# A four-layer transformer on one core: attention heads that add rotated halves in the contraction, another loading order at the start, and sums of exponentials on GpSimd

## The reference, cut to what matters

```
def apply_rope(x, cos, sin):
    half = x.shape[-1] // 2
    x1, x2 = x[..., :half], x[..., half:]
    return jnp.concatenate([x1 * cos - x2 * sin, x1 * sin + x2 * cos], axis=-1).astype(x.dtype)
...
        s = (jnp.einsum('bqhd,bkhd->bhqk', qn_b, k_nope)
             + jnp.einsum('bqhd,bkd->bhqk', qr_b, k_rope)).astype(jnp.float32) * scale
```

```
    s = jnp.einsum("bshd,bmhd->bhsm", q, k).astype(jnp.float32) * (1.0 / math.sqrt(XA_HD))
    p = jax.nn.softmax(s, axis=-1)
    o = jnp.einsum("bhsm,bmhd->bshd", p.astype(v.dtype), v)
```

## Time and profile before

| | us |
|---|---|
| median of 3 runs (lowest, highest) | 2482.35 (2479.43, 2487.03) |
| the profiled execution | 2481.47 |
| its span, first to last instruction | 2479.7 |
| PE busy | 2331.0 (94%) |
| POOL busy | 1661.9 (67%) |
| DVE busy | 1051.8 (42%) |
| ACT busy | 501.6 (20%) |

### The profile page before, as it was taken

One profiled execution on the slowest core, in us unless ns is written; L12 is line 12 of the kernel. 1 busy time (PEld: TensorE's weight loads), 2 busy tenths in 40 slices (PEclk: granted clock), 3 DMA queues, 4 the chain that ended last, 5 costly groups with the idle time before them and its releaser, 6 DMA issues.

```text
span 2479.7 us, 29722 instructions
## 1 busy us (share of the span) xinstructions
PE 2331.0 (94%) x11040; PEld 1901.3 (77%) x11040; DVE 1051.8 (42%) x1342; ACT 501.6 (20%) x955; POOL 1661.9 (67%) x1370
## 2 busy tenths in 40 slices
PE   5968999999996899999999699999999898999999
PEld 4766788888876678888887468888888776888887
DVE  7664533322366344332237545215334333540430
ACT  3245211110134521111012521001111263100000
POOL 5466677767756667777777577767766564776774
PEclk9988999999998899999999899999999999999999
DMA  4300122222330012222232112222232200222222
GB/s 145 107 27 18 68 102 95 91 87 93 117 107 18 18 69 102 97 89 87 94 124 102 52 68 88 99 102 96 91 119 86 86 35 17 85 102 102 85 102 85
DMA packets 37844, 207.93 MB, mean 84 GB/s; under 512 B 3532, under 2 KB 10316, under 8 KB 16888
## 3 DMA queue, kind: packets, MB, share of 16 engines
q1 hardware_dynamic: 37752, 206.70, 23.9%
HBM read 204.55 MB, written 2.13 MB: 83 GB/s over the span
## 4 chain that ended last, share of the span: by engine, by line
PE 60%; DVE 2%; POOL 2%; ACT 2%; issue 1%; DVEq 0%; POOLq 0%; ACTq 0%
PE ps L821 18%; PE ps L826 18%; PE ps L825 18%; POOL wl L649 1%; PE ps L1185 1%; PE ps L1159 1%; ACT rt L1335 1%; POOL wh L643 0%; PE ps L1160 0%; PE ps L1163 0%; PE ps L1161 0%; DVE sq L1705 0%; DVE t L1713 0%; DVE nt L1705 0%; PE ps L1200 0%
## 5 line engine op out<-in xcount | busy, mean ns | idle before, releaser
L649 POOL TENSOR_TENSOR wl<-raw,wh 128x512 fp32r<-128x512 f32 (+1 forms) x776 | 1032.8, 1361 | 0.0
L643 POOL TENSOR_SCALAR wh<-raw 128x1024 fp32r<-128x1024 f32 (+1 forms) x388 | 427.3, 1121 | 595.3 <-PE ps L821 462.6
L821 PE MATMUL ps<-h,wh 128*128 128x512 f32 x1576 | 618.1, 392 | 18.4 <-POOL wl L649 9.2
L825 PE MATMUL ps<-h,wh 128*128 128x512 f32 x1576 | 615.2, 390 | 0.0
L826 PE MATMUL ps<-h,wl 128*128 128x512 f32 x1576 | 615.1, 390 | 0.0
L821 PE MATMUL ps<-act,wh 128*128 128x512 f32 x1120 | 437.6, 391 | 1.1 <-DVE x L1705 1.1
L825 PE MATMUL ps<-act,wh 128*128 128x512 f32 x1120 | 436.0, 389 | 0.0
L826 PE MATMUL ps<-act,wl 128*128 128x512 f32 x1120 | 436.0, 389 | 0.0
L821 PEld LDWEIGHTS ps<-h,wh 128*128 128x128 f32 x1576 | 297.0, 188 | 85.5 <-issue 24.4
L825 PEld LDWEIGHTS ps<-h,wh 128*128 128x128 f32 x1576 | 296.9, 188 | 62.3 <-issue 1.0
L826 PEld LDWEIGHTS ps<-h,wl 128*128 128x128 f32 x1576 | 297.0, 188 | 62.1
(11 more groups left out here) (337 smaller groups left out, 2681.8 us busy)
## 6 DMA issues: line engine op xcount, KB each, us to landing
raw<-w_gu SPq DMA_DIRECT2D x44, 1024.0 KB, 4.8
raw<-w_up SPq DMA_DIRECT2D x32, 1024.0 KB, 4.8
raw<-w_down_b SPq DMA_DIRECT2D x32, 1024.0 KB, 4.8
raw<-w_down_a SPq DMA_DIRECT2D x32, 704.0 KB, 4.0
raw<-w_in_a SPq DMA_DIRECT2D x14, 1024.0 KB, 4.9
raw<-w_in_f SPq DMA_DIRECT2D x13, 1024.0 KB, 4.8
raw<-w_in_r SPq DMA_DIRECT2D x11, 1024.0 KB, 4.8
raw<-w_out_a SPq DMA_DIRECT2D x8, 1024.0 KB, 7.6
```

The costliest lines, as they stand in the source:

```text
L643: pool.tensor_scalar(hi_s[:, part], raw[s][:, part], 1.0, 1.0, ALU.mult, ALU.mult).then_inc(hi_done, 1)
L649: ins = pool.tensor_tensor(lo_s[:, part], raw[s][:, part], hi_s[:, part].bitcast(F32), ALU.subtract)
L821: first = pe.matmul(out, w_hi, v_hi, start=start, stop=False)
L825: pe.matmul(out, w_hi, v_lo, start=False, stop=False)
```

## The change

Four things are changed.

1. MLA queries keep 128 rows: one multiplication by `cgq` on all rows, no addition. The key's 32 rotated rows stand twice in the 128-row key tiles, so the score matmul adds the two products. One copy (`krp`) is added per layer, and the four zero fills of the key tiles at the start of MLA are gone.
2. High part and rest of a key are one tile `key` of 128x1024, so a zero fill of both is one instruction where SWA and FOX still need it.
3. At the start SP issues `vec`, then the first weight chunk, then `x` in four parts, then the constants, the small tables and the second chunk. ACT makes the row tiles first and copies the constants behind them. POOL splits the first chunk by halves (`half_ready` after the first), and PE's small products for the bias table stand behind `lead_pair`.
4. In XA, POOL adds the two halves of the exponentials (`summed`), and PE multiplies that sum with the ones: one float32 matmul instead of two. POOL's `mixed` of an earlier head stands ahead of the splitting of a chunk in these heads.

```
-                halves = (slice(0, n // 2), slice(n // 2, n))
...
+                if early:
+                    for half in range(2):
+                        pool.wait_ge(hi_done, high(half))
+                        low(2 * half).then_inc(hi_done, 1)
+                        low(2 * half + 1).then_inc(w_ready if half else half_ready, 1)
+                        hi.up()
...
+            def summed(hd):
+                if hd >= 2:
+                    pool.wait_ge(ready[5], bk.filled(5, hd - 2))
+                for b in (2, 3):
+                    pool.wait_ge(free[b], bk.emptied(b, hd))
+                pt = pts["xa"][hd % 2]
+                pool.tensor_tensor(pt_sum[hd % 2], pt[:, 0:T], pt[:, T:2 * T], ALU.add).then_inc(sum_ready, 1)
...
+                    if m.name == "xa":
+                        if hd >= 2:
+                            mixed(m.vrow(hd - 2), m.tile(hd - 2))
+                        if hd < m.heads:
+                            summed(hd)
                     if hd == chunk_at:
 
                         split_all(1, BLOCKS)
...
-                        for j in range(keys):
-                            last = pe.matmul(ps[5][:, :], ones[:, :], pt[:, j * T:(j + 1) * T],
-                                             start=j == 0, stop=j == keys - 1)
-                        last.then_inc(ready[5], 1)
+                        pe.wait_ge(sum_ready, sumr.up())
+                        pe.matmul(ps[5][:, :], ones[:, :], pt_sum[hd % 2], start=True, stop=True).then_inc(ready[5], 1)
...
+                tsc(krp[96:P, :], krp[64:96, :], 1.0)
...
-                    tt(qc[0:96, i, :], ps[b][0:96, :], cgq[0:96, :], ALU.mult)
-                    tt(ts[64:96, :], ps[b][96:P, :], cgq[96:P, :], ALU.mult, bk.empties(b, u))
-                    tt(qc[64:96, i, :], qc[64:96, i, :], ts[64:96, :], ALU.add)
+                    tt(qc[:, i, :], ps[b][:, :], cgq[:, :], ALU.mult, bk.empties(b, u))
...
-                    for s in range(2):
-                        zero(kh[s], slice(96, P))
-                        zero(kl[s], slice(96, P))
-                    r = slice(64, 96)
+                    r = slice(64, P)
                     tt(ts[r, :], krp[r, :], ps[7][r, :], ALU.mult, bk.empties(7, 0))
```

More of the change, by code:

```diff
@@ L435, in build @@
         free = [sem(f"free{b}") for b in range(8)]
-        ld_x, ld_vec, ld_cst, ld_pos = sem("ld_x"), sem("ld_vec"), sem("ld_cst"), sem("ld_pos")
+        ld_x = [sem(f"ld_x{i}") for i in range(KT // 2)]
+        ld_vec, ld_cst, ld_pos = sem("ld_vec"), sem("ld_cst"), sem("ld_pos")
+        half_ready = sem("half_ready")
         ld_hot = sem("ld_hot")
@@ L624, in _, with split @@
             g = 0
-            def split(s, nblk, first=False, slot_done=None):
+            def split(s, nblk, first=False, slot_done=None, early=False):
                 full[s].n += 16
@@ L905, in claim, with bias_rows, in_a @@
                 return tt % 4
-            pe.wait_ge(consts_ready, 1)
-            pe.wait_ge(ld_relb, 16)
-            pe.wait_ge(ld_hot, 16)
-            for half in range(2):
-                pe.matmul(ps[4 + half][0:SWA_HEADS, 0:384], relb[0:32, 0:SWA_HEADS],
-                          cst[0:32, C_HOT + 384 * half:C_HOT + 384 * (half + 1)],
-                          start=True, stop=True).then_inc(ready[4 + half], 1)
-            bk.close({4: 1, 5: 1})
-            def in_a():
+            def bias_rows():
+                pe.wait_ge(consts_ready, 1)
+                pe.wait_ge(ld_relb, 16)
+                pe.wait_ge(ld_hot, 16)
+                for half in range(2):
+                    pe.matmul(ps[4 + half][0:SWA_HEADS, 0:384], relb[0:32, 0:SWA_HEADS],
+                              cst[0:32, C_HOT + 384 * half:C_HOT + 384 * (half + 1)],
+                              start=True, stop=True).then_inc(ready[4 + half], 1)
+                bk.close({4: 1, 5: 1})
+            def in_a(first):
                 lead_pair(claim(0), claim(1), chunk())
+                if first:
+                    bias_rows()
                 norm_sums(True)
@@ L1372, in square_rows @@
                 hr.n += 1
+            sc.wait_ge(ld_vec, 16)
+            for k in range(KT):
+                sc.wait_ge(ld_x[k // 2], 16)
+                if k >= 2:
+                    sc.wait_ge(h_ready, hr.at(-1))
+                fn(h[:, k, 0, :], x[:, k, :], ACT.Copy, scale=col("attn0", k)).then_inc(h_hi_ready, 1)
+                fn(sq[:, k % 2, :], x[:, k, :], ACT.Square).then_inc(square_ready, 1)
+                hr.n += 1
             sc.wait_ge(ld_cst, 16)
-            sc.wait_ge(ld_vec, 16)
             for dst, c0 in ((ident, C_IDENT), (ones, C_ONES), (ident_r, C_IDENT), (anti_r, C_ANTI), (neg_ones_r, C_ONES),
@@ L1382, in _ @@
             last.then_inc(consts_ready, 1)
-            sc.wait_ge(ld_x, 16)
-            for k in range(KT):
-                if k >= 2:
-                    sc.wait_ge(h_ready, hr.at(-1))
-                fn(h[:, k, 0, :], x[:, k, :], ACT.Copy, scale=col("attn0", k)).then_inc(h_hi_ready, 1)
-                fn(sq[:, k % 2, :], x[:, k, :], ACT.Square).then_inc(square_ready, 1)
-                hr.n += 1
             sc.wait_ge(turns_ready, 1)
```

108 lines of the change are left out of this document (60 added, 48 removed).

## The result

The changed kernel takes 2466.74 us (median of 6 runs, 2464.09 to 2474.36); the one before, with three more runs beside it, 2481.76 (2479.43 to 2487.24). The ratio is 0.9940 (0.9929 to 0.9951): 15.0 us less, where 21.7 were forecast. The executions of one kernel are not alike: the six of the changed kernel have mean granted clocks of 0.979 (the shortest, 2464.09) down to 0.970 (the longest, 2474.36). So a stage length read from one trace is that of one execution.

The account below looks back on a forecast made before the run. PE's matmuls carry 60% of the chain, so only places where PE waits can give time. Terms 5.0 + 6.2 + 5.2 + 0.4 + 3.4 + 1.5 = 21.7 off 2481.47 gave 2459.8 us, range 2452 to 2472.

Parts of the forecast that it names:

- rival 1: XA: POOL's sums cost what they save, 0.5 in layer F and 1.5 lost in R; 2465.7 us, chance 0.16.
- rival 2: Layers 0 and 1: POOL's windows take all the MLA query gain, DVE is early and waits; 2466.0 us, chance 0.12.
- rival 4: Start: the new order gains nothing, `cq` is waited for until 55.67 as before; 2464.8 us, chance 0.07.
- A: Start: new loading order and split first chunk bring tile 4 earlier; 5.0 us gained (2.7 to 6.5).
- B: MLA queries, layers 0 and 1: 12 DVE instructions go, POOL's windows hold most; 3.1 us per layer, 6.2 (3 to 8).
- Rival 3: Layers 0 and 1: POOL's windows don't hold, POOL too is freed; 7.3 us per layer, 2451.4, chance 0.06.
- C: Start of MLA: four zero fills leave DVE's queue ahead of `ts`; 2.6 us per layer, 5.2 (4.8 to 6).
- E: XA in layer F: one half of the matmuls with the ones goes, four heads; 3.4 us (0.5 to 3.5).
- F: XA in layer R: same removal, but sums collide with DVE's recurrence; 1.5 us gained (-1.5 to 3.5).
- FOX: FOX: eight zero fills become four of double width; 0.4 us gained (nothing to 1.3).
- (5): Weight blocks behind the broken lead: TensorE stays at 1.2 GHz, kernel slower than before; 2488.6 us, chance 0.02.

Follow-up runs that it names:

- start_only: Kernel before with only the third edit (loading order, first chunk split by halves, bias products behind the lead): 2477.34 us, ratio 0.9982.
- xa_only: Kernel before with only the fourth edit (sums of exponentials on POOL, split results ahead of the chunk): 2477.00 us, ratio 0.9988.
- mla_only: Kernel before with only the first two edits (128-row MLA queries, joined key tiles, no zero fills at MLA's start): 2474.94 us, ratio 0.9976.
- before_filled: Kernel before with all the filling matmuls of best: 2476.03 us, ratio 0.9982.
- prep_between: Changed kernel with POOL's preparation `ql` of the second pair of SWA heads moved between the two window sets: 2469.51 us, ratio 0.9942.
- warm_all: warm_mla with more filling matmuls ahead of SWA's score columns, behind the last MLA head and at FOX's start: 2462.09 us, ratio 0.9914.
- fills_back: Changed kernel with four fills of 32x512 put back ahead of MLA's first `ts`: 2469.18 us, ratio 0.9935.
- warm_mla: Changed kernel with 25 filling matmuls per layer of kind A ahead of the waits at MLA's start: 2462.50 us, ratio 0.9929.
- best: Changed kernel with warm_mla's filling, 8 more behind MLA's and XA's last heads, 6 behind FOX's, layer R's sums on PE: 2452.58 us, ratio 0.9874.
- changed_again: Changed kernel run once more, unaltered, for a second trace: 2466.05 us, ratio 0.9948.
- r_pe_sum: Changed kernel with layer R's sums of exponentials on PE again: 2464.40 us, ratio 0.9926.

## Why the prediction was right, and where its sizes were off

The forecast 2459.8 was 6.9 below the median and the range 2452 to 2472 held it; the direction was right. The time by itself proves little of the mechanism: 2466.74 lies nearer to rival 1 (2465.7), rival 2 (2466.0) and rival 4 (2464.8) than to the forecast, and only the rows below tell them apart. Some of it was luck: the profiled difference of 13.6 holds 1.7 at the start and 2.1 in layer R's inputs that no step of the prediction had and that come and go with TensorE's level; in layer F the level took 1.5 back. By terms:

**A, 5.0: measured 5.5 (5.8 alone) in the traces, 4.4 by start_only's median.** POOL began on the first chunk at 6.55 (6.0 forecast), DVE at 10.69 (10.3), the eighth row ended at 30.15 (30.6), the stall of 2.31 went. The lead ended 1.1 later than I took it, as the seventh row was done at 28.64 and not at 27.3; the lead's last 30 matmuls took 9.0 from there, near the 9.2 forecast, and the first nine of them did run 0.43 apart. So tile 4 came 55.67 - 51.88 = 3.8 earlier. The other 1.7 no step had: before, the wait of 2.31 was followed by 8 matmuls at the low level. They are gone with the wait, but they are also absent in xa_only, mla_only and before_filled, which have the wait: against those traces the new start gains about 4. Before, from tile 4 to `cqn`:

```profile
55.60:74.90 19.30, 19.21 (x77) 14.04 (x78) 14.75 (x15) 6.09 (x10) 10.97 (x9) 0.91 0.16 54
```

and after:

```profile
51.80:69.40 17.60, 17.59 (x79) 12.86 (x78) 14.55 (x15) 4.19 (x7) 11.16 (x9) 1.00 0.23 89
```

**B, 3.1 per layer: 3.2 and 3.1 at the first SWA result.** The first maxima came 7.2 earlier than the shift of the start, 7.3 forecast, and GpSimd's windows took 4 back, as forecast; prep_between and warm_all show that it is that queue. Both parts of the 3.1 are there: the maxima behind `t` start 0.15 after `t` ends instead of 1.6, and POOL's queue from the first `ql` to the second takes 25.3 instead of 27.3, 2.0 less (1.6 forecast). Rival 3 and with it the full effect of the rule in the Trainium skill, "SBUF — State Buffer", section "Who interferes with whom", did not come about, though single rows agree with the rule: DVE's key rest, two inputs in SBUF, is 1.64 beside POOL's split and 0.69 without. Of instructions with two inputs the section says only that they contend; "for the whole instruction" stands there for DVE's two-port modes. POOL won 2.0 per layer, not 6.8. The prediction's reckoning by that rule also mixes its figures: 13.6 is twice 6.8, already below twice 7.3, so rival 3's 30.1 is no cut of 29.1.

**C, 2.6 per layer: 1.6 and 2.0.** This is the term that was mis-sized, and the step is "4 x 0.65 = 2.6 of PE's 5.66, so DVE still is what PE waits for". DVE still was, and the wait fell from 5.66 to 3.07 as forecast; but right behind it, without the fills, DVE's first key rest falls on POOL's split of the fifth SWA result and takes 0.95 longer (fills_back). I had not asked what else ran on POOL at that moment.

**The sum.** B and C together were to stay: 11.4 in two layers. 4.8 and 5.1 arrived at MLA's first heads, less 1.7 that layer 0 lost in the later SWA heads; the residuals kept -0.9 and 3.9. In layer 0, 2.2 went in the MLA heads and 1.7 at the output projection, PE's granted clock being 0.87 and 0.92 there against 0.95 and 1.00. That the level is the cause of these two is shown by warm_mla and best, which do the same work plus filling in 44.55 and 20.23. The prediction treated an earlier start as a gain that stays; it named the level only as a rival behind the lead. The 1.7 of the later SWA heads is the level too. In layer 0 of the changed kernel the score columns of head 2, behind a PE wait of 1.68, fall to 0.21 apart after the first seven matmuls:

```profile
145.63 0.41 PE L1201 MATMUL ps<-ql,key 128*128 128x256 f32 x1
145.85 0.42 PE L1202 MATMUL ps<-qh,key 128*128 128x256 f32 x1
```

and in best, with the same code there and no filling, behind a wait of 0.25, they stay at 0.12:

```profile
145.84 0.28 PE L1210 MATMUL ps<-ql,key 128*128 128x256 f32 x1
145.96 0.28 PE L1211 MATMUL ps<-qh,key 128*128 128x256 f32 x1
```

The slow columns lie across the first SWA result, where the table cuts, so a clock of 0.98 for the stage hides them. In changed_again, warm_mla and r_pe_sum the columns are slow too and the stage takes 25.3; in mla_only, prep_between and best they are not, and it takes 23.6.

**E, 3.4: 3.4,** in the changed kernel and in xa_only (2.5 in the traces of r_pe_sum and fills_back, whose code there is the same); heads 4.98 apart instead of 5.84. **F, 1.5: 0.3,** and -0.9 in xa_only, with the sums themselves costing about 0.9: it lies between the forecast and the bound -1.5, by the mechanism given for that bound. **FOX, 0.4: -0.7** with layer F's inputs; 1.5 of it is a stretch of weight blocks, which no edit touched, at a lower level. The same sort of thing paid 2.1 in the inputs of layer R: the stage is as short in start_only and mla_only and as long as before in xa_only, prep_between and fills_back, and no edit touched it. **Rivals:** of (1) the sums' cost in R was seen, but R as a whole did not lose 1.5 and F paid in full; (2), (3) and (4) did not come about. Of (5) only the level was seen: the lead's matmuls were back at 0.23 after the first ten, and the low level came later, in the heads.

## What to carry to other kernels

A saved wait is a gain at its place only; follow it to the next point where all engines meet, and expect part of it to be taken or doubled there by TensorE's level. Before an instruction is removed as dead weight, look at what the next one will run beside. In a kernel with short broken stretches between long rows of matmuls, filling the waits on TensorE with matmuls into a bank that is about to be overwritten can be worth as much as a tuned change: best, with layer R's sums on PE again, is 14.2 us below the changed kernel, and 1.26% below the one before. But the same filling in the kernel before gave only 4.3, so such filling has to be tried at each place. And read a stage in more than one trace before giving it a price: here the same code differed by 1 to 2 us from trace to trace.

## What the runs showed of the hardware that I had not expected

In the trace of before the granted clock fell some time after a wait, not in it: tile 4's first four matmuls behind the 2.31 of waiting are 0.23 apart, and the next eight 0.43. In three other traces of the same start the clock did not fall there at all. Two traces of the changed kernel agree in the length of every stage of layers 0 and 1 to 0.1 us, levels included, while r_pe_sum, the same program up to layer R, differs by 1.8 in one of them; and six executions of the changed kernel differ by 10 us, the longer the lower their mean granted clock (0.979 to 0.970). Filling does not work everywhere: where the next stage waits for another engine's queue (SWA) it gave nothing, and warm_all, with filling in FOX, has the last products of layer F's heads at the low level, 3.1 us worse.
